# Attention layer of a decoder trunk: index scores and logits as fp32r products over stacked high and low halves, heads in pairs

## The reference

```python
parts = split_cols(h @ w_in, [SC_WIDTH] * 3 + [ATT_WIDTH] * 3 + [IDX_HEADS * IDX_DIM, IDX_DIM, IDX_HEADS])
sc_b, sc_c, sc_x, q, k, v, q_idx, k_idx, w_idx = parts
y_conv = sc_b * causal_depthwise_conv(sc_c * sc_x, conv_w)
# q, k, q_idx, k_idx: rope on the first 16 of 64 channels
score = jax.nn.relu(jnp.einsum('bthd,bsd->bths', qib, k_idx))
score = jnp.einsum('bths,bth->bts', score, wb).astype(jnp.float32)
score = jnp.where(admissible[None], score, -jnp.inf)
_, sel = lax.top_k(score, top_k)                    # top_k = 128
logits = jnp.einsum('bthd,btkhd->bthk', qb, k_sel).astype(jnp.float32) * scale
probs = jax.nn.softmax(jnp.where(valid, logits, -jnp.inf), axis=-1).astype(v.dtype)
y = jnp.einsum('bthk,btkhd->bthd', probs, v_sel)    # then concatenated with y_conv, @ w_out
```

## Time and profile before

| | us |
|---|---|
| median of three executions | 2181.73 (2180.53 to 2186.84) |
| the profiled execution | 2181.9, span 2179.9 |
| attention layer, units 1 to 28, in the profile | 385.5 to 647.5 |
| TensorE busy in the span | 2131.8 |
| VectorE, ScalarE, GpSimd busy | 1052.7, 775.1, 285.7 |
| mean granted TensorE clock | 0.994 |

### The profile page before, as it was taken

One profiled execution on the slowest core, in us unless ns is written; L12 is line 12 of the kernel. 1 busy time (PEld: TensorE's weight loads), 2 busy tenths in 40 slices (PEclk: granted clock), 3 DMA queues, 4 the chain that ended last, 5 costly groups with the idle time before them and its releaser, 6 DMA issues.

```text
span 2179.9 us, 25816 instructions
## 1 busy us (share of the span) xinstructions
PE 2131.8 (98%) x9608; PEld 1704.5 (78%) x9608; DVE 1052.7 (48%) x1574; ACT 775.1 (36%) x1098; POOL 285.7 (13%) x379
## 2 busy tenths in 40 slices
PE   7999999999999999999999999998999999999997
PEld 6888888756667888888788888877788887888886
DVE  4444444678744444433344442355666554444422
ACT  4333322223553333322333332244655543333221
POOL 1000000113121000000000000025656210000001
PEclk9999999999999999999999999999999999999999
DMA  5333322212112223332233332222222223333321
GB/s 171 97 97 97 113 93 66 87 49 68 49 46 90 89 97 96 104 103 90 79 98 96 97 112 98 84 75 66 78 78 60 75 87 96 97 96 96 107 95 50
DMA packets 57036, 192.00 MB, mean 88 GB/s; under 512 B 11872, under 2 KB 11904, under 8 KB 56960
## 3 DMA queue, kind: packets, MB, share of 16 engines
q1 hardware_dynamic: 54752, 190.85, 27.8%
q10 hardware_dynamic: 2208, 0.13, 0.1%
HBM read 188.58 MB, written 2.38 MB: 88 GB/s over the span
## 4 chain that ended last, share of the span: by engine, by line
PE 86%; POOL 4%; DMA 3%; DVE 3%; ACT 2%; issue 1%; SPq 1%; DVEq 0%; POOLq 0%; ACTq 0%
PE prod L454 27%; PE prod L456 26%; PE prod L455 26%; DMA blk<-blocks 2%; POOL rows_tmp L1527 2%; POOL rows L1530 2%; PE misc L658 1%; PE misc L587 1%; PE prod L544 1%; PE misc L605 1%; ACT w_hi L801 1%; DVE w_lo L1070 1%; PE misc L567 0%; DMA blocks<-a_mat 0%; SPq L422 0%
## 5 line engine op out<-in xcount | busy, mean ns | idle before, releaser
L1070 DVE TENSOR_TENSOR w_lo<-raw,w_hi 128x1024 fp32r<-128x1024 f32 (+1 forms) x300 | 400.4, 1335 | 790.2 <-ACT w_hi L801 789.6
L454 PE MATMUL prod<-h_hi,w_hi 128*128 128x512 f32 x1856 | 753.0, 406 | 1.2 <-DVE w_lo L1070 0.9
L456 PE MATMUL prod<-h_hi,w_lo 128*128 128x512 f32 x1856 | 726.6, 391 | 0.0
L455 PE MATMUL prod<-h_lo,w_hi 128*128 128x512 f32 x1856 | 725.5, 391 | 0.0
L801 ACT ACTIVATE w_hi<-raw 128x1024 fp32r<-128x1024 f32 (+1 forms) x317 | 356.3, 1124 | 604.8 <-PE prod L456 593.2
L454 PEld LDWEIGHTS prod<-h_hi,w_hi 128*128 128x128 f32 x1856 | 350.2, 189 | 102.4 <-issue 34.2
L456 PEld LDWEIGHTS prod<-h_hi,w_lo 128*128 128x128 f32 x1856 | 349.5, 188 | 74.6
L455 PEld LDWEIGHTS prod<-h_lo,w_hi 128*128 128x128 f32 x1856 | 350.3, 189 | 69.3 <-issue 4.3
L456 PE MATMUL prod<-a_hi,w_lo 128*128 128x512 f32 x704 | 278.2, 395 | 0.0
L454 PE MATMUL prod<-a_hi,w_hi 128*128 128x512 f32 x704 | 278.2, 395 | 0.0
L455 PE MATMUL prod<-a_lo,w_hi 128*128 128x512 f32 x704 | 278.2, 395 | 0.0
(11 more groups left out here) (234 smaller groups left out, 1809.6 us busy)
## 6 DMA issues: line engine op xcount, KB each, us to landing
raw<-in_w SPq DMA_DIRECT2D x253, 512.0 KB, 3.5
raw<-in_wd SPq DMA_DIRECT2D x64, 704.0 KB, 4.1
blk<-blocks SPq DMA_DIRECT2D x8, 512.0 KB
x<-in_x SPq DMA_DIRECT2D x8, 256.0 KB, 5.4
out<-y_out SPq DMA_DIRECT2D x8, 256.0 KB, 2.2
silu_g<-g_rows SPq DMA_DIRECT2D x7, 256.0 KB, 4.4
consts<-in_consts SPq DMA_DIRECT2D x1, 768.0 KB, 8.1
blocks<-a_mat SPq DMA_DIRECT2D x40, 4.0 KB, 1.4
```

Source lines behind the costliest of these rows:

```text
L454: pe.matmul(bank, wh, hi, start=first and k == 0, stop=False)
L455: pe.matmul(bank, wh, lo, start=False, stop=False)
L456: ins = pe.matmul(bank, wl, hi, start=False, stop=last and k == tiles_n - 1)
L1070: dve.tensor_tensor(w_lo[:, n % 2, 0:w], raw[:, n % 4, 0:w], w_hi[:, n % 2, 0:w].bitcast(F32), ALU.subtract).then_inc(lo_ready, 1)
```

## The change

Index queries, index keys, queries and keys are split into a high fp32r part and a remainder. The two halves of a head (64 rows each) are stacked to 128 rows for the queries (`stack`, in emix_hi and emix_lo, not yet in use), by SBUF to SBUF DMAs on SP's queue; the keys stand twice, high part and remainder, over both halves (`ik_dup`, `k_dup`). A product is then two fp32r matmuls over 128 rows. Heads go in pairs: 12 pairs of scores (slots 3 and 6 from unit 8), 16 of attention, one each five slots, with one value product for both heads. VectorE multiplies the tables by rstd once, evacuates a roped unit with two multiplies (cosine, sine), and adds the rotation; ScalarE rounds at k = 7, GpSimd subtracts. GpSimd also takes the weight remainders from unit 4 on (before: 14). The final split of the attention output is done pair by pair in the last block. Top-k rounds are placed anew; some tensors share memory.

```diff
+PAIRS = HEADS // 2
+
+
 def ev_extras():
 
-    idx = [("idx", b, h) for b in range(1, TT) for h in range(HEADS)]
+    idx = [("idx", b, j) for b in range(1, TT) for j in range(PAIRS)]
     top = [("top", b, r) for b in range(1, TT) for r in range(ROUNDS)]
     out = {}
     for u in range(len(EV_UNITS)):
-        for k in (1, 4, 6):
-            if u >= 6 and idx:
+        for k in (3, 6):
+            if u >= 8 and idx:
                 out[u * KT + k] = [idx.pop(0)]
-        for k in (2, 5, 7):
-            if u >= 9 and top:
+        for k in (2, 4, 5, 7) if 14 <= u < 18 else (2, 5, 7):
+            if u >= 10 and top:
                 out[u * KT + k] = [top.pop(0)]
     assert not idx and not top
     return out
...
-POOL_UNIT = 14
+POOL_UNIT = 4
 
 
 
 ATT_SLOT = 17 * KT + 6
-ATT_STEPS = {"logits": 0, "scale": 2, "turn": 4, "values": 6}
+ATT_STEPS = {"logits": 0, "scale": 3, "turn": 5, "values": 8, "mix": 10}
...
-    for q in range(Q_ITEMS):
+    for p in range(ATT_PAIRS):
         for step, at in ATT_STEPS.items():
-            out.setdefault(ATT_SLOT + q * slots // Q_ITEMS + at, []).append((step, q))
+            out.setdefault(ATT_SLOT + p * slots // ATT_PAIRS + at, []).append((step, p))
...
+STACK_LAG = 5
+IDX_PAIRS, ATT_PAIRS = (TT - 1) * PAIRS, TT * PAIRS
+STACKED = 16 * 4
...
-        iq, qT, kT = ev("iq", [4, T]), ev("qT", [4, T]), ev("kT", [4, T])
-        ik = ev("ik", [T])
+        k_dup = ev("k_dup", [HEADS, 2, T], F32R)
+        y_f = nc.alloc_sbuf_tensor_at("y_f", [P, 4, T], F32, offset=ev.at)
+        cosT, sinT = ev("cosT", [T]), ev("sinT", [T])
+        ik_dup = ev("ik_dup", [2, T], F32R)
...
+        cbuf, ubuf = ev("cbuf", [T]), sq_acc
+        score3 = ev("score3", [T])
+        score = {1: raw[:, 0, KT * P:KT * P + 2 * P], 2: raw[:, 1, KT * P:KT * P + 3 * P], 3: score3[:]}
+        relu_s = sq
         probs = silu_g
+        split_hl = (silu_g, act_f)
         probsT = ev("probsT", [2, TT, P])
+        relu_of = (sq[:], probsT[:].rearrange("p e t c -> p e (t c)"))
...
+        def stack(kind, h):
+            return (emix_hi, emix_lo)[h % 2][:, (0 if kind == "iq" else 4) + h // 2, :]
...
+                v = u - STACK_LAG
+                if 1 <= v < len(EV_UNITS) and EV_UNITS[v][0] in ROPED:
+                    kind, m = EV_UNITS[v]
+                    pair = split_hl[v % 2]
+                    sp.wait_ge(rlo_ready, v + 1)
+                    for e in range(2):
+                        rows_e = slice(HD * e, HD * e + HD)
+                        for half in range(2):
+                            rows_h = slice(HD * half, HD * half + HD)
+                            if kind == "k":
+                                sp.dma_start(k_dup[rows_h, 2 * m + e].bitcast(F32), pair[rows_e, :, :])\
+                                    .then_inc(stacked[v % 2], 16)
+                            else:
+                                sp.dma_start(stack(kind, 2 * m + e)[rows_h].bitcast(F32), pair[rows_e, half, :])\
+                                    .then_inc(stacked[v % 2], 16)
...
-            def idx_pe(b, h):
-                q = (b - 1) * HEADS + h
-                if b == 1 and h == 0:
-                    pe.wait_ge(roped, 5)
-                if q >= 2:
-                    pe.wait_ge(relu_done, q - 1)
-                r = slice(HD * (h % 2), HD * (h % 2) + HD)
+            def idx_pe(b, j):
+                p = (b - 1) * PAIRS + j
+                if p == 0:
+                    pe.wait_ge(rlo_ready, 1)
+                    pe.wait_ge(stacked[0], 2 * STACKED)
+                    pe.wait_ge(stacked[1], 2 * STACKED)
+                else:
+                    pe.wait_ge(relu_done, p)
                 w = (b + 1) * P
-                pe.matmul(prod[:, 1 + 2 * (q % 2), 0:w], iq[r, h // 2, b * P:(b + 1) * P], ik[r, 0:w],
-                          start=True, stop=True).then_inc(idx_mm, 1)
+                for e in range(2):
+                    for part in range(2):
+                        ins = pe.matmul(misc[:, 1 + e, 0:w], stack("iq", 2 * j + e)[:, b * P:(b + 1) * P],
+                                        ik_dup[:, part, 0:w], start=part == 0, stop=part == 1)
+                ins.then_inc(idx_mm, 1)
...
+            def att_logits(p):
+                b, j = p // PAIRS, p % PAIRS
+                if p == 0:
                     pe.wait_ge(roped, N_SIDE)
-                if q >= 2:
-                    pe.wait_ge(masked, q - 1)
+                    pe.wait_ge(stacked[0], 6 * STACKED)
+                    pe.wait_ge(stacked[1], 6 * STACKED)
+                else:
+                    pe.wait_ge(masked, p)
                 w = (b + 1) * P
-                pe.matmul(misc[:, q % 2, 0:w], qT[r, h // 2, b * P:(b + 1) * P], kT[r, h // 2, 0:w],
-                          start=True, stop=True).then_inc(logit_mm, 1)
-
...
+                for e in range(2):
+                    for part in range(2):
+                        ins = pe.matmul(prod[:, 1 + 2 * e, 0:w], stack("q", 2 * j + e)[:, b * P:(b + 1) * P],
+                                        k_dup[:, 2 * j + e, part, 0:w], start=part == 0, stop=part == 1)
+                ins.then_inc(logit_mm, 1)
...
+            def att_pv(p):
+                b, j = p // PAIRS, p % PAIRS
+                pe.wait_ge(probsT_ready, p + 1)
+                if p >= 1:
+                    pe.wait_ge(y_taken, p)
                 for c in range(b + 1):
...
-                    ins = pe.matmul(misc[r, 3, 0:P], vtok[:, c, h // 2, r.start:r.stop], probsT[:, q % 2, c, :],
-                                    start=c == 0, stop=c == b)
+                    ins = pe.matmul(misc[:, 3, 0:2 * P].rearrange("p (e c) -> p e c", e=2), vtok[:, c, j, :],
+                                    probsT[:, :, c, :], start=c == 0, stop=c == b)
...
+                        act.activation(relu_of[p % 2][:, :, 0:w], misc[:, 1:3, 0:w], ACT.Relu).then_inc(relu_done, 1)
...
+                elif step == "turn":
+                    act.wait_ge(turned, p + 1)
+                    if p >= 1:
+                        act.wait_ge(pv_done, p)
+                    else:
+                        act.wait_ge(idx_added, 2 * IDX_PAIRS)
+                    act.activation(probsT[:].rearrange("p e t c -> p e (t c)")[:, :, 0:w], misc[:, 1:3, 0:w], ACT.Copy)\
+                        .then_inc(probsT_ready, 1)
                 elif step == "values":
-                    b, h = q // HEADS, q % HEADS
-                    r = slice(HD * (h % 2), HD * (h % 2) + HD)
-                    act.wait_ge(pv_done, q + 1)
-                    act.activation(y_f[r, h // 2, b * P:(b + 1) * P], misc[r, 3, 0:P], ACT.Copy).then_inc(y_taken, 1)
...
+                    act.wait_ge(pv_done, p + 1)
+                    for e in range(2):
+                        r = slice(HD * e, HD * e + HD)
+                        ins = act.activation(y_f[r, j, b * P:(b + 1) * P], misc[r, 3, e * P:(e + 1) * P], ACT.Copy)
+                    ins.then_inc(y_taken, 1)
+                    if b == TT - 1:
+                        act.wait_ge(y_taken, p + 1)
+                        act.activation(emix_hi[:, 4 + j, :], y_f[:, j, :], ACT.Copy).then_inc(att_hi, 1)
...
-            act.wait_ge(y_taken, Q_ITEMS)
-            for m in range(4):
-                act.activation(emix_hi[:, 4 + m, :], y_f[:, m, :], ACT.Copy).then_inc(emhi, 1)
+                    if k == KT - 1 and (kind == "ik" or kind in ROPED):
+                        act.wait_ge(roped, u)
+                        pair = split_hl[(u - 1) % 2]
+                        hi_of = ik_dup[:, 0, :] if kind == "ik" else pair[:, 0, :].bitcast(F32R)
+                        act.activation(hi_of, pair[:, 1, :], ACT.Copy).then_inc(rhi_ready, 1)
...
+                    link(dve.tensor_tensor(cosT[:], cosT[:], rstd[:], ALU.mult))
+                    link(dve.tensor_tensor(sinT[:], sinT[:], rstd[:], ALU.mult))
                 elif kind in ROPED:
-                    dst = {"iq": iq, "q": qT, "k": kT}[kind][:, m, :]
+                    dst = split_hl[u % 2][:, 1, :]
                     dve.wait_ge(rot_done, u + 1)
-                    link(dve.tensor_tensor(ubuf[:], misc[:, 0, :], sinT[:], ALU.mult))
-                    dve.wait_ge(cos_part, u)
-                    dve.tensor_tensor(dst, dst, ubuf[:], ALU.add).then_inc(roped, 1)
+                    dve.wait_ge(evac, EV_S + u + 1)
+                    dve.tensor_tensor(dst, dst, misc[:, 0, :], ALU.add).then_inc(roped, 1)
...
+                        if kind in ROPED:
+                            if u == 2:
+                                dve.wait_ge(rlo_ready, 1)
+                            elif u >= 3:
+                                dve.wait_ge(stacked[u % 2], STACKED * ((u - 1) // 2))
+                            dve.tensor_tensor(split_hl[u % 2][:, 1, :], bank, cosT[:], ALU.mult)
+                            dve.tensor_tensor(roped_in[:, u % 2, :], bank, sinT[:], ALU.mult).then_inc(evac, 1)
+                        else:
```

(41 more changed lines are left out.)

149 lines of the change are left out of this document (62 added, 87 removed).

## The result

Over 20 runs the changed kernel takes **2185.7 us** (median; 2183.3 to 2190.1), the kernel before 2183.0 on the same chips: 1.0016 times as long, 95% interval 1.0009 to 1.0023. That is "the same" by the 0.3% of the prediction, and above its range. The profiled execution has a span of 2184.1 us, 4.2 more than before.

The account below looks back on a forecast made before the run. The prediction took TensorE, busy 98% of the span, to bound the kernel: 2181.9 - 41 + 2.2 (start) + 8.5 (units 10 to 13) + 1.2 (units 14 to 17) + 12 (attention) + 0.5 (transfers) = 2165 us, range 2148 to 2180.

Parts of the forecast that it names:

- TensorE's saving: Index scores, logits and value products: cheaper fp32r pairs save 16.7 + 19.8 + 5.8 = 42 us, less 1: 41.
- rival (d): Scores and logits: fp32r narrower than 512 columns runs at the float32 rate, 26.5 us more, 2181 us; chance 0.04.
- Start: After the first rope: VectorE's extra multiplies delay the evacuation that rotation 1 waits for; TensorE stands 2.2 us.
- Units 10 to 13: Rope units: a closed loop of evacuation, rotation, scores, relu and adds makes TensorE wait; 8.5 us including slow adds, 0 to 13.
- Contention: VectorE's adds in units 10 to 13, slowed beside GpSimd: 16 at a mean excess of 0.1 to 0.2, 2 to 3 us.
- rival (c): Units 11 to 14 and attention: waits keep TensorE at half clock; slower beyond 34 us of it, 2190 at 50; chance 0.06.
- Its own sign of being wrong: Inside the layer: matmuls of 0.42 us appearing there would show the forecast wrong.
- Units 14 to 17: Units with four top-k rounds: VectorE's 4 x 1.23 + 1.4 = 6.3 us against TensorE's 5.9; 1.2 us lost.
- Attention: 16 pairs at five slots: TensorE waits through ScalarE's order and VectorE's load; 12 us, from 4 to 22.
- Transfers: Stacking DMAs of roped units: nearly covered, 0.5 us lost; at the upper end the four key units lose 8 to 10.
- End: Last units' chain to emix_lo, which held TensorE 2.26 us, and the halved clock behind it: untouched, nothing.
- Rival (b): Rope units and attention: key transfers near 13 us and loops at upper bounds eat the saving; about 2176 to 2184; chance 0.14.

Follow-up runs that it names:

- e13: Changed kernel with one score pair per unit at slot 1 of units 7 to 18 and value products at slot 6, mix at 10: 2160.7 us.
- e4: Changed kernel plus eight unused 512-column products ahead of the rotations or transposes of units 2 and 10 to 14: 4.4 us faster than it by the ratios.
- e12: Changed kernel, score pairs at slots 1 and 4, POOL_UNIT 14, values at 6, eight unused products in units 2 and 10 to 14; total time not stated.
- e14: e13 with POOL_UNIT 14 and the unused products before rotation 1 (unit 2) alone: 2.0 us over e13 by the ratios, 3.1 by the medians.
- e1: Changed kernel with one score pair per unit, at slot 6 of units 6 to 17, instead of two from unit 8: 2196.7 us.
- e5: Changed kernel with score pairs at slots 1 and 4 instead of 3 and 6: 15.5 us faster than it by the ratios.
- e9: Changed kernel with one score pair per unit, at slot 1 of units 6 to 17: 2169.7 us.
- e3: Changed kernel with the weight remainders of units 4 to 13 back on VectorE instead of GpSimd: 7.6 us faster than it by the ratios.
- e7: Changed kernel with attention's value products at slot 6 instead of 8, mix left at 10: 4.8 us faster than it by the ratios.
- e6: Changed kernel without the indexer's top-k rounds (max and match_replace): time inside its expected 2162-2170 us.
- e11: Changed kernel with each stacking transfer issued a second time, to an unread DRAM scratch: 9 us slower than it by the medians.
- e2: Changed kernel with value products at slot 6 and mix at 8, which also shifted the later pairs' spacing: no gain in time.

## Why the prediction was wrong

It named the right direction of the terms in its sum and lost on their size, and it put the clock at nothing. Layer: -41 + 24.4 was forecast, -41 + 45 came.

- **TensorE's saving, 41 us**: right as far as it can be seen. The pairs cost what was said, rival (d) fell, and with the waits mostly gone (e13) the rope stage takes 107.7 us where 121.4 - 16.7 = 104.7 would be full.
- **Start, +2.2**: 2.0 of wait, as worked out, and 1.6 of half clock behind it, which the filling of e4, e12 and e14 gives back. Measured 3.9.
- **Units 10 to 13, +8.5 (0 to 13)**: the step that failed. The rope stage lost 23.9. I had closed a loop from rotation over the first score pair to the adds, and filled it with durations of VectorE at rest. e1 breaks that loop and nothing is won; e5 keeps the pairs' distance and moves them off the unit's end, and 14.8 come back. What TensorE waits for is the order at the end of a unit: ReLU of the pair at slot 6, its adds, then the evacuation. e1 against e9 shows it with one pair per unit at either place: 133.3 and 112.4 us.
- **Contention, 2 to 3 of those 8.5**: mis-sized. I took a mean excess of 0.1 to 0.2 us per add, since an add rarely met GpSimd before. The change itself ties them: the high-half copy that releases GpSimd stands right behind the ReLU that releases the adds. One small add per block paid 2.0, the pair 1.1. e3 prices it at 7.1 in this order, and at nothing in a better one.
- **Clock**: rival (c) asked for over 34 us at the lower level and got 0.06. It was wrong to hold it as a rival alone: seven of the stands inside the layer were followed by a clock of 0.57 to 0.63, some 1.6 us each. Of the 45 us lost, 35.2 are waits, and seven times 1.6 is about the rest, an estimate from these windows. It is shown by experiment only at the start (e4, e12, e14). The prediction put waits of 0.3 to 2 us at no such price. That of 1.97 had it, and those that came were up to 4.6. Its own sign of being wrong, matmuls 0.42 apart inside the layer, was there: 0.43 from 401.25 to 404.23.
- **Units 14 to 17, +1.2**: 4.3 for the one wait at unit 14, part of the 23.9. It isn't the four rounds that were counted, but the same order once more: the adds of the last pair (2.46), its neg_future add (2.31) and a round stand ahead of the evacuation. e5 keeps 3.9 of it behind the same slow adds; e9, which has no pair at the end of a unit, has 2.3 in three waits.
- **Attention, +12 (4 to 22)**: 18.1, inside the bounds. The parts named are there: the scaling behind the values' copy (e7, 4.5 us) and VectorE's rounds ahead of the reciprocal (e6, 9.8). The two aren't a sum, and what remains of the loss in e13 isn't told apart.
- **Transfers, +0.5**: right as far as the waits show; none of TensorE's in the changed kernel is put down to them. e11 shows that the upper end, 8 to 10, was real for twice the traffic.
- **End, 0**: right. The 2.26 us before the first output tile are 2.24 in the changed kernel (at 656.45, with a clock of 0.57 in the 4 us behind it) and 2.2 in every experiment but e2, which has 3.3.

Rival (b), "the waits eat it", was nearest to the outcome, and in part for the wrong reason: it took 13 us of key transfers, which had no part in it, and 13 for the loop, where the rope stage lost 23.9.

## What to carry to other kernels

When TensorE gets lighter, go through the other engines in program order at each unit's end and ask which instruction, released late, stands ahead of the one that TensorE needs next; then move the late one, a slot or two is enough. Where a change hands elementwise work to GpSimd, look at what releases it: if the same event releases a VectorE instruction with two SBUF inputs, count GpSimd's whole instruction, not a mean. And add to a wait of TensorE what the clock may cost behind it: 1.6 us behind one of 2.0 here (e4), and a clock near 0.6 for 4 us behind all of those of 2.4 to 4.6 in the changed kernel.

## What was not expected of the hardware

- A VectorE add of 128 columns and two SBUF inputs took 2.33 us instead of 0.29 beside a GpSimd subtraction of 2.54, at the same place in the changed kernel, e1 and e6. It took 0.29 there in e5, where the two don't meet, and in e3, where the subtraction isn't on GpSimd.
- TensorE's half clock can be bought off with useless products: eight of 512 columns ahead of rotation 1 brought the clock of 396:405 us from 0.81 to 1.00, and the way to unit 3 from 7.9 us to 6.4 (e4, e12, e14). The window in the changed kernel, then in e12:

```profile
396.00:405.00 9.00, 7.03 (x23) 4.96 (x22) 5.58 (x8) 2.21 (x3) 2.92 (x2) 0.81 0.05 19
```
```profile
396.00:405.00 9.00, 8.79 (x37) 6.62 (x36) 6.76 (x11) 2.54 (x4) 2.97 (x2) 1.00 0.12 50
```

- A stand of TensorE of 2.12 us was followed by a granted clock of 1.00 and one of 1.97 by 0.63 (both in the changed kernel), so here the length alone doesn't tell which.
- An SBUF to SBUF transfer of 256 KB over 64 partitions lands in 4.2 to 4.4 us, longer than a plain load of 512 KB in the same stretch, 385 to 520 us (changed kernel, DMA issues: count, size, median to landing):

```profile
raw<-in_w SPq DMA_DIRECT2D x15, 512.0 KB, 3.9
k_dup<-act_f SPq DMA_DIRECT2D x8, 256.0 KB, 4.2
k_dup<-silu_g SPq DMA_DIRECT2D x8, 256.0 KB, 4.4
emix_hi<-act_f SPq DMA_DIRECT2D x8, 128.0 KB, 2.3
```
